# One stage in place of three between the first expert layer and the second projection of a two-layer diffusion backbone, with a shorter routing and a reordered scan end

## The chip, the cores and the metric

The kernel runs on one core of one Trainium2 chip, in float32 throughout. The metric is the device time of one execution in microseconds. TensorE, VectorE (DVE in the rows), ScalarE (ACT), GpSimd (POOL) and SyncE (SP) each run their own instruction stream and meet at semaphores. PE in the rows is TensorE's matmul, PEld its weight load. SyncE only issues transfers here; GpSimd issues the indirect ones (gathers) and ScalarE a few.

## What is computed

Two layers over 256 context tokens and 1024 latent tokens (1280, in ten tiles of 128), width 1024. What matters here of the reference:

```
# end of layer 0, tokens = context and latent
out = hier_moe(tokens, ...)          # every token: 2 of 32 experts, sorted and padded by expert
h = h + g2 * out                     # g2: a gate row of 1024, one for context, one for latent

# begin of layer 1
a = modulate(rmsnorm(h, norm_mix[1]), sh1, s1)      # rmsnorm(h) * (1 + s1) + sh1
q, k, v = split_qkv(a @ w_in)        # 1024 x 1536; context tokens: k and v only (512 columns)
q, k = axial_rope(q), axial_rope(k)  # latent tokens only
```

`hier_moe` picks a group of experts and two experts in it per token, weighs them, and evaluates each expert on its own tokens. The delta rule scan of layer 0 (`gated_delta_rule`) goes over the tiles in both directions at once, with a triangular inverse per tile and head; its values are `v_new = T (beta v - beta e^g k S)` and its state grows by `k^T (v_new * decay)`.

## The kernel before

`build` (L2499) runs stages in sequence. Each is a block: all engines start together after a barrier and end together before the next; ahead of the barrier GpSimd sets each semaphore of the new block. The order of the stages is `begin`, `norm_mod`, `project0`, `delta_scan`, `gate_heads`, `project_norm`, then `moe` (`route`, `experts`, `combine`), `norm_mod` again, `project1`, `attend`, `project_norm`, and `moe` for layer 1. The hidden state `H` stays in SBUF.

**Between the experts and attention** three blocks follow one another.

- `combine` (L1949), layer 0: for each of the ten tiles GpSimd gathers the two expert rows of every token (L1983, two gathers of 512 KB per tile, all twenty issued at once into ten buffers), ScalarE scales one (L2003), VectorE adds the other (L2031), multiplies by the gate row (L2033) and adds to `H` (L2038, on odd tiles GpSimd does it, L1987). ScalarE squares `H` with a row sum (L1999). After the last tile one mean, one root and one reciprocal serve all ten tiles (L2051 to L2053).
- `norm_mod` (L312): SyncE spreads the scale and shift rows over the partitions (L308) and loads the 6 MB of `at_w_in` (L145). Per tile VectorE makes `H * rstd * scale` (L362) and adds the shift (L365), TensorE turns it with eight transposes (L379), and ScalarE copies two half tiles to `aT`, which holds all ten tiles (L351).
- `project1` (L2072): per tile TensorE multiplies `aT` by the weights (L2136; group 2 alone for the two context tiles, groups 0, 1 and 2 for a latent tile), then turns the tile before (L2151, four transposes per group). ScalarE copies the turned tile (L2166), then the products to `z` (L2179) and the keys twice (L2190). VectorE (L2207 to L2209) and GpSimd (L2220 to L2222) rotate. SyncE stores `att_q`, `att_k` and `att_v`.

**Routing** (`route`, L1464, once per layer) is one chain on VectorE, in which each instruction waits for the one before (`st.link`). It begins when `const_ramp` has come from memory (L1504, L1554). It finds group and experts, counts by two matmuls (L1528, L1529), runs over the tiles with a position and a running count each (L1590, L1591), and finds units, slots and the rows of each block (L1594 to L1620), from which TensorE makes the index list (L1532). Meanwhile VectorE builds the table of blocks, on all partitions alike, with wide comparisons (L1624 to L1653), and copies the list (L1655). ScalarE has by then issued the 12 MB of the first two experts. `experts` starts with a gather by that list, and its further weight loads wait for the blocks that use their buffers.

**The scan** (`delta_scan`) has ten steps, with both directions `d` interleaved. Each has five merges in 64-blocks and a sixth across. What follows the merges on VectorE: `state_times_beta` and `residual` for both directions (L1003, L1008), `decay_beta` (L975), the decayed values out of PSUM (L1070) once ScalarE has copied `v_new` (L943), and `a_matrix` (L980). TensorE multiplies `TT` by `R` for both directions, then keys by keys for both (all at L1093), and turns A of the next step (`turn_a`, L1109, L1112) when `at_ready` and `vd_ready` allow.

## Time and profile before

| | us |
|---|---|
| median of 3 runs | 3668.06 (3665.86 to 3669.89) |
| the profiled execution | 3672.49 |
| its span, first to last instruction | 3670.8 |
| TensorE busy in the span | 3018.0 (82%) |
| VectorE, ScalarE, GpSimd busy | 1216.2, 676.9, 332.2 |
| mean granted TensorE clock | 0.921 |

Since the stages stand in sequence, a stage's own slowest chain sets its length, and busy shares over the whole span say little. The stages are told apart by the first and last instruction of their lines in the order of time.

### The profile page before, as it was taken

Reading aid. Unit: us, or ns where it says so; the run is one execution under the profiler, and the core shown is the slowest. Engines: PE = TensorE matmul, PEld = TensorE weight load, DVE = VectorE, ACT = ScalarE, POOL = GpSimd, SP = SyncE. Lnnn points to the kernel's source line nnn. Section 1 sums busy time; section 2 is a strip of 40 time slices with the busy share of each in tenths; the row PEclk is TensorE's granted clock in tenths of the full one; section 3 lists DMA queues with packets and bytes.
Section 4 is the critical chain, followed back from the end, with each engine's and each line's share of the span. In section 5 each row is a group of like instructions: output and inputs, shape, how many; then the busy total and the mean of one; then the engine's idle time right before and its main releaser. Section 6 shows DMA issues by size and latency. Waiting matters only on the chain. (4 is left out here: it accounts for less than half of the span.)

```text
span 3670.8 us, 51018 instructions
## 1 busy us (share of the span) xinstructions
PE 3018.0 (82%) x18238; PEld 1569.6 (43%) x18239; DVE 1216.2 (33%) x2215; ACT 676.9 (18%) x1522; POOL 332.2 (9%) x374
## 2 busy tenths in 40 slices
PE   3999998899949939999998549868889489789991
PEld 1555554788824423333333124445555333233330
DVE  3323322766672351111110242256643501001114
ACT  2312211111120100000000131156651000000002
POOL 0000001111210010000000212201110000000002
PEclk8999999999979959999999769989999699899995
DMA  6511101232236348679978330131110389886874
GB/s 273 157 50 57 50 26 50 88 97 80 66 138 220 143 181 355 272 307 378 369 290 352 143 116 35 45 123 42 52 31 35 155 343 398 331 369 248 353 291 166
DMA packets 153503, 667.47 MB, mean 182 GB/s; under 512 B 26480, under 2 KB 62864, under 8 KB 122624
## 3 DMA queue, kind: packets, MB, share of 16 engines
q1 hardware_dynamic: 125360, 545.54, 38.7%
q0 software_dynamic: 18496, 66.64, 4.9%
q10 hardware_dynamic: 9488, 53.09, 3.5%
q8 instruction: 109, 1.79, 0.2%
q14 instruction: 50, 0.41, 0.0%
HBM read 595.84 MB, written 69.39 MB: 181 GB/s over the span
## 5 line engine op out<-in xcount | busy, mean ns | idle before, releaser
L1831 PE MATMUL bank<-w,xT 128*64 x3392 | 751.5, 601 | 66.4 <-DMA w<-in_moe_w 40.8
L511 PE MATMUL bank<-aT,w 128*128 128x512 f32 (+1 forms) x1344 | 487.8, 523 | 6.7 <-DVE short L712 5.9
L1831 PEld LDWEIGHTS bank<-w,xT 128*64 128x64 f32 x3392 | 249.1, 139 | 532.6 <-issue 532.5
L1851 PE MATMUL bank<-w,hT 128*64 (+1 forms) x1696 | 380.9, 602 | 55.2 <-issue 50.0
L511 PEld LDWEIGHTS bank<-aT,w 128*128 128x128 f32 x1344 | 255.1, 191 | 227.6 <-issue 215.8
L1923 DVE TENSOR_TENSOR h<-h,bank 128x512 f32<-128x512 f32 x53 | 36.5, 688 | 785.2 <-PE bank L1831 785.2
L1851 PEld LDWEIGHTS bank<-w,hT 128*64 128x64 f32 x1696 | 122.2, 138 | 277.7 <-issue 277.7
L2136 PE MATMUL bank<-at_w_in,aT 128*128 128x512 f32 x416 | 182.3, 598 | 2.9 <-PEq L116 2.9
L2328 PE MATMUL bank<-eye,probs 128*128 128x128 f32 x640 | 99.1, 286 | 45.2 <-ACT probsT L2394 45.0
L1780 POOL DMA_INDIRECT x<-moe_x,idx_block x55 | 53.4, 970 | 841.0 <-PE bank L1807 839.3
L2136 PEld LDWEIGHTS bank<-at_w_in,aT 128*128 128x128 f32 x416 | 79.2, 192 | 99.8 <-issue 99.8
L1890 ACT COPY xT<-bank 128x512 f32<-128x512 f32 x55 | 32.2, 585 | 482.6 <-PE bank L1807 482.6
L1883 ACT ACTIVATE h<-bank 128x512 f32<-128x512 f32 x53 | 31.6, 597 | 470.4 <-PE bank L1831 470.4
L1350 PE MATMUL bank<-at_w_out,att 128*128 128x512 f32 x256 | 112.6, 599 | 3.0 <-PEq L116 3.0
L379 PE MATMUL bank<-eye,a 128*128 128x128 f32 x160 | 31.7, 368 | 100.7 <-DVE a L365 96.1
L1934 DVE COPY y<-bank 128x512 f32<-128x512 f32 x53 | 36.6, 691 | 223.3 <-PE bank L1851 223.3
L1896 ACT COPY y<-bank 128x512 f32<-128x512 f32 x53 | 31.0, 585 | 420.6 <-PE bank L1851 420.6
L2328 PEld LDWEIGHTS bank<-eye,probs 128*128 128x128 f32 x640 | 68.5, 142 | 82.0 <-ACT probsT L2394 60.5
L1929 DVE COPY hT<-bank 128x512 f32<-128x512 f32 x53 | 36.7, 692 | 194.0 <-PE bank L1813 194.0
L1350 PE MATMUL bank<-ab_w_out,oT 128*128 128x512 f32 x160 | 77.1, 627 | 24.5 <-PEq L116 24.5
L1807 PE MATMUL bank<-eye,x 128*128 128x128 f32 x440 | 65.4, 293 | 34.1 <-DMA x<-moe_x,idx_block 34.1
L1047 DVE TENSOR_TENSOR T_TT_sub<-T_TT_sub,bank 128x512 f32<-128x512 f32 x100 | 68.7, 688 | 73.6 <-PE bank L1171 73.6
(336 smaller groups left out, 3919.3 us busy)
## 6 DMA issues: line engine op xcount, KB each, us to landing
w<-in_moe_w SPq DMA_DIRECT2D x180, 2048.0 KB, 13.2
ada_w<-in_ada_w SPq DMA_DIRECT2D x48, 1024.0 KB, 8.6
moe_y<-y ACTq DMA_DIRECT2D x53, 512.0 KB, 10.4
w<-in_moe_w ACTq DMA_DIRECT2D x12, 2048.0 KB, 21.5
w<-in_ab_w_in SPq DMA_DIRECT2D x28, 512.0 KB, 3.9
moe_y<-zero POOLq DMA_DIRECT2D x1, 8192.0 KB, 24.9
moe_x<-a SPq DMA_DIRECT2D x13, 512.0 KB, 2.7
at_w_in<-in_at_w_in SPq DMA_DIRECT2D x3, 2048.0 KB, 16.6
```

The source lines that it names most:

```text
L511: mm = pe.matmul(k.bank[3 * s + n][:, 0:width], w[j][:, c, :], aT[:, c, at:at + width], start=(c == 0), stop=(c == KC - 1))
L1047: V_.tensor_tensor(X[d][:], X[d][:], both_new[d], ALU.subtract).then_inc(x_ready[d], 1)
L1350: mm = pe.matmul(k.bank[Y[n % 2] + half][:], lhs(c, t), w[:, c, half * 512:(half + 1) * 512], start=(c == 0), stop=(c == KC - 1))
L1780: pool.indirect_dma_start(x[:], None, dr["moe_x"], bass.IndirectOffsetOnAxis(ap=one[:, 0:1], axis=0)).then_inc(x_in, 16)
L1807: t = pe.transpose(k.bank[X[c // 4]][:, (c % 4) * P:(c % 4 + 1) * P], x[:, c:D:KC], k.eye[:])
L1831: mm = pe.matmul(k.bank[UP[half]][u * UNIT:(u + 1) * UNIT, :], xT[:, c, u * UNIT:(u + 1) * UNIT], w13[:, r if u else ds(buf[0], 1), half, ...
L1851: mm = pe.matmul(k.bank[Y[half]][u * UNIT:(u + 1) * UNIT, :], hT[:, c, u * UNIT:(u + 1) * UNIT], w2[:, r if u else ds(buf[0], 1), at:at + ...
L1923: nc.vector.tensor_tensor(h[:], h[:], k.bank[UP[1]][:], ALU.mult).then_inc(h_ready, 1)
L1929: nc.vector.tensor_copy(hT[:].rearrange("p c q -> p (c q)"), k.bank[HT][:]).then_inc(hT_ready, 1)
L1934: nc.vector.tensor_copy(y[:, 0:512], k.bank[Y[0]][:]).then_inc(y_dve, 1)
L2136: mm = pe.matmul(k.bank[3 * s + g][:], aT[:, c, t * P:(t + 1) * P], w[:, c, g * 512:(g + 1) * 512], start=(c == 0), stop=(c == KC - 1))
L2328: mm = pe.transpose(k.bank[6 + f % 2][:, at:at + P], pr[m % 2][:, h, c * P:(c + 1) * P], k.eye[:])
```

## The change

Three parts, and one load that moves to `begin`: the ramp is loaded there once and kept.

```diff
@@ begin: SyncE
         sp.dma_start(k.tri[:], ...).then_inc(consts_in, 16)
+        sp.dma_start(k.ramp[:], dr["const_ramp"].to_broadcast([P, P])).then_inc(consts_in, 16)
```

**Scan ends.** The decayed values move into the merges of the next step and read ScalarE's copy; one direction's residual moves into the last merge; two loops over the directions become one each.

```diff
+        def decayed_values(s, d):
+            dve.wait_ge(vn_copied[d], primed(s + 1))
+            V_.tensor_tensor(VD[d][:], VN[d][:], stat(kdec, ...), ALU.mult).then_inc(vd_ready[d], 1)
@@ VectorE, merge n of step s
+                if n == 0 and s:            # before the two subtractions of merge 0
+                    decayed_values(s - 1, 0)
                 if n == 4:
                     decayed_scores(s, 0)
+                    state_times_beta(s, 0)
                 for d in R2:
                     ...subtract(X[d])
+                    if n == 4 and d == 0:
+                        residual(s, 0)
+                if n == 0 and s:            # after them
+                    decayed_values(s - 1, 1)
@@ VectorE, after the merges
-            for d in R2:
-                state_times_beta(s, d)
-                residual(s, d)
+            state_times_beta(s, 1)
+            residual(s, 1)
             for d in R2:
                 if more:
                     decay_beta(s + 1, d)
-            for d in R2:
-                dve.wait_ge(vn_copied[d], primed(s + 1))
-                V_.tensor_tensor(VD[d][:], bank[d][P_BANK], ...).then_inc(vd_ready[d], 1)
-            for d in R2:
-                if more:
                     a_matrix(s + 1, d)
@@ TensorE
         def turn_a(s, d):
-            pe.wait_ge(vd_ready[d], primed(s))
+            pe.wait_ge(vn_copied[d], primed(s))
...
                 heads(bank[d][P_BANK], TT[d], R[d]).then_inc(vn_ready[d], 1)
-            for d in R2:
                 if s + 1 < NT:
                     key_products(s + 1, d)
```

**Routing.** No load ahead; the running counts are linked alone and the positions come from one instruction; the table is computed with one unit per partition and turned by five matmuls; the weights of the experts are computed later.

```diff
         for t in range(T):
-            st.link(V.tensor_tensor(pos[:, t], k.bank[0][...], run[:], ALU.add))
-            st.link(V.tensor_tensor(run[:], run[:], k.bank[1][...], ALU.add))
+            st.link(V.tensor_tensor(run[:, t + 1, :], run[:, t, :], k.bank[1][...], ALU.add))
+        V.tensor_tensor(pos[:], run[:, 0:T, :], k.bank[0][...], ALU.add)
@@ after at_row: L1624 to L1653 go; in their place, on [P, NE], [P, 1] and [P, 3, 11]
+        V.tensor_scalar(begun[:], incl[:], unit[:, 1:2], None, ALU.is_gt)
+        st.link(V.tensor_scalar(cmp[:], incl[:], unit[:, 0:1], None, ALU.is_le))
+        st.link(V.tensor_reduce(own[:], cmp[:], AX.X, ALU.add))
+        ...four more..., then_inc(units_owned, 1)
+        ...the six instructions L1579 to L1584, moved here...
         dve.wait_ge(listed, primed(1))
         V.tensor_copy(idx[:], k.bank[4][:, 0:NB])
+        dve.wait_ge(tabled, primed(1))
+        ...seven short copies out of banks 5 and 6 to table[0:1, ...]
@@ TensorE, after the index list
+        pe.wait_ge(units_owned, primed(1))
+        for n in range(1 + RING):
+            pe.matmul(k.bank[5][0:1, n * P:(n + 1) * P], of_unit[:, n:n + 1], k.eye[:], ...)
+        pe.matmul(k.bank[6][0:1, 0:NE], ones[:, 0:1], begun[:], ...).then_inc(tabled, 1)
```

**The joined stage.** `combine_project` takes the place of layer 0's `combine`, of `norm_mod` and of `project1`, tile by tile. Layer 1 keeps `combine`.

```diff
+    RY = 3                               # gathered tiles held
@@ SyncE, in this order: rope, two gate rows, then
+        sp.dma_start(w[:, :, 1024:1536], src[:, :, 1024:1536]).then_inc(w_in[2], 16)
+        for v in R2:
+            for n, m in enumerate((1, 0)):
+                sp.dma_start(cols[:, v, n, :], dr["mods"][1, v, m * D:(m + 1) * D].rearrange("(c p) -> p c", p=P),
+                             allow_slow_non_contiguous=True).then_inc(cols_in, 16)
+        ...w groups 0 and 1
@@ TensorE, project(t)
+            pe.wait_ge(aT_act, primed(t + 1)); pe.wait_ge(aT_dve, primed(t + 1))
+            for n, g in enumerate(groups(t)):
+                pe.wait_ge(w_in[g], primed(16))
                 ...eight products into bank 3 * s + g...
+                if n == 0 and t + 1 < NT:
+                    turn_a(t + 1)        # eight transposes, banks 6 and 7
@@ ScalarE, for t in -2 .. NT-1
+            scale(t + 2)                 # as L2003
+            copy_a(t + 1)                # four [P, 128] Identity with scale and bias columns, first waits cols_in
+            square(t + 2)                # Square with row sum, then waits mean_ready, Sqrt
             take_turned(t - 1); take_products(t); double_keys(t)
@@ VectorE, for t in -2 .. NT
+            rotate(t - 1)                # L2207 to L2209
+            add(t + 2)                   # L2031, L2033, L2038
+            copy_a(t + 1)                # four [P, 128] tensor_scalar out of PSUM
+            normalise(t + 2)             # mean, reciprocal, a = H * rstd
@@ GpSimd
+        gathers of tiles 0, 1, 2, then for t in -2 .. NT
+            rotate(t - 1)                # L2220 to L2222
+            gather(t + 5) once sum_ready(t + 2)
```

## Rows read from the trace of the kernel before

**Rows 1.** The page: its span, and the granted clock in 40 slices.

```profile
span 3670.8 us, 51018 instructions
PEclk8999999999979959999999769989999699899995
```

**Rows 2.** Timeline from combine to project1: start, length, engine, line, idle time before.

```profile
2081.96 0.80 SPq L308 DMA_DIRECT2D gate_rows<-mods  x2
...
2090.65 1.15 ACT L2003 ACTIVATE y<-y,weights 128x1024 f32<-128x1024 f32 x1 [13.23 <-DMA y<-moe_y,slots]
...
2136.64 0.22 DVE L2053 RECIPROCAL rstd<-rstd 128x10 f32<-128x10 f32 x1 [1.35 <-ACT rstd L2018]
...
2176.75 16.19 PE L2136 MATMUL bank<-at_w_in,aT 128*128 128x512 f32 x32 [2.90 <-PEq L116]
...
2193.22 20.77 PE L2136 MATMUL bank<-at_w_in,aT 128*128 128x512 f32 x48
...
2214.25 20.77 PE L2136 MATMUL bank<-at_w_in,aT 128*128 128x512 f32 x48
...
2236.68 13.90 PE L2136 MATMUL bank<-at_w_in,aT 128*128 128x512 f32 x32
```

**Rows 3.** Groups by line, 2081.9 to 2391 us: busy time, mean ns, idle before.

```profile
L2031 DVE SCALAR_TENSOR_TENSOR y<-y,weights 128x1024 f32<-128x1024 f32 x10 | 12.8, 1284 | 22.2 <-ACT y L2003 22.2
L365 DVE TENSOR_TENSOR a<-a,shift_rows 128x1024 f32<-128x1024 f32 x10 | 12.3, 1225 | 0.3
L351 ACT COPY aT<-bank 128x512 f32<-128x512 f32 x20 | 10.7, 589 | 27.6 <-PE bank L379 27.6
L1999 ACT ACTIVATE squares<-H 128x1024 f32<-128x1024 f32 x10 | 10.5, 1049 | 18.0 <-POOL H L1987 16.7 <-DVE H L2038 1.2
```

**Rows 4.** The tile conv_qkv: a one-input VectorE operation, and its loads.

```profile
L666 DVE TENSOR_SCALAR y<-x_raw,conv_qkv x12: 882/884/891, 122.8 to 571.5; 128x1282 f32<-128x1282 f32 x12
...
L448 SPq DMA_DIRECT2D conv_qkv<-in_ab_conv_qkv x3: 583/1335/5400, 92.5 to 108.7; - x3
...
DMA to landing us min/median/max: 5.0/10.1/21.1
```

**Rows 5.** Stretches: length, busy PE, PEld, DVE, ACT, POOL, clock, DMA share, GB/s.

```profile
2093.00:2096.00 3.00, 0.00 (x0) 0.00 (x0) 2.93 (x4) 1.39 (x2) 2.39 (x3) 0.50 1.03 418
...
2913.00:2918.00 5.00, 5.00 (x26) 5.00 (x25) 4.83 (x6) 0.00 (x0) 0.00 (x0) 0.50 0.16 69
```

**Rows 6.** Timeline of the routing of layer 0, GpSimd, VectorE and TensorE.

```profile
1308.65 0.20 POOL L1508 MEMSET ones<- 128x128 f32 x1 [17.17 <-POOLq L116]
...
1314.80 0.23 DVE L1555 TENSOR_SCALAR w<-w 128x128 f32<-128x128 f32 x1 [15.49 <-DMA w<-in_const_ramp]
...
1325.99 0.09 DVE L1588 MEMSET w<- 128x32 f32 x1 [1.37 <-PE bank L1529]
...
1330.79 0.82 DVE L1594 TENSOR_TENSOR w<-w 128x640 f32<-128x640 f32 x1
...
1343.30 8.75 PE L1532 MATMUL bank<-w,at_row 128*128 128x37 f32 x40 [17.46 <-DVE at_row L1620]
...
1360.47 0.20 DVE L1655 CAST idx<-bank 128x37 int32<-128x37 f32 x1
```

**Rows 7.** The same of layer 1, where it differs.

```profile
2911.94 7.05 PE L1532 MATMUL bank<-w,at_row 128*128 128x37 f32 x32 [15.08 <-DVE at_row L1620]
...
2929.12 0.20 DVE L1655 CAST idx<-bank 128x37 int32<-128x37 f32 x1
```

**Rows 8.** TensorE at the end of a scan step, timeline; VectorE's merges, 654 to 1030 us, by line.

```profile
713.16 1.09 PE L1195 MATMUL bank<-T_TT_sub,A_T_off 64*64 64x64 f32 x16 [0.33 <-DVE A_T_off L1061]
714.84 1.16 PE L1093 MATMUL bank<-R,TT 128*128 128x128 f32 x8 [0.58 <-DVE R L1008]
...
719.41 0.68 PE L1109 MATMUL bank<-eye,AT 64*64 64x64 f32 x16 [0.30 <-DVE AT L980]
...
L1047 DVE TENSOR_TENSOR T_TT_sub<-T_TT_sub,bank 128x512 f32<-128x512 f32 x100 | 68.7, 688 | 73.6 <-PE bank L1171 73.6
```

More of the change, by code:

```diff
@@ L1500, in route @@
     block = k.block()
-    @block.sync
-    def _(sp):
-        sp.dma_start(ramp[:], dr["const_ramp"].to_broadcast([P, P])).then_inc(c_in, 16)
     @block.gpsimd
@@ L1647, in _ @@
-        per = tf[:, Table.OF_BLOCK:].rearrange("p (b n) -> p b n", n=Table.PER)
-        st.link(V.scalar_tensor_tensor(out=owner[:], in0=rounds[:, 0], scalar=-float(RING), in1=owner[:], op0=ALU.mult, op1=ALU.add))
-        st.link(V.tensor_scalar(per[:, :, 0:2], owner[:].rearrange("p (b u) -> p b u", u=2), float(RING), None, ALU.add))
-        for r in range(RING):
-            st.link(V.tensor_copy(per[:, :, 2 + r], rounds[:, r, 1:U:2]))
-        st.link(V.tensor_copy(table[:], tf[:]))
+        dve.wait_ge(units_set, primed(1))
@@ L1659 @@
+        V.tensor_copy(table[0:1, Table.BLOCKS:Table.BLOCKS + 1], k.bank[6][0:1, NE - 1:NE])
+        V.tensor_scalar(table[0:1, Table.LAST:Table.LAST + 1], k.bank[6][0:1, NE - 1:NE], -1.0, None, ALU.add)
 class Ring:
@@ L1945, in _, with combine @@
         second(last)
-def combine(k, l, first, slots, wts, final=False):
+def combine(k, l, first, slots, wts):
     nc, dr, H = k.nc, k.dram, k.H
@@ L2067, in moe, with combine_project @@
         with k.scope():
-            combine(k, l, first, slots, wts, final=(l == 1))
-def project1(k, aT, weights):
-    nc, dr = k.nc, k.dram
+            after(slots, wts)
+def combine_project(k, slots, wts):
+    nc, dr, H = k.nc, k.dram, k.H
     R2 = range(2)
@@ L2097, in rounds, with groups, turn_bank, wait_bank @@
         return t if t < CT else CT + 3 * (t - CT)
+    def groups(t):
+        return (2,) if t < CT else (0, 1, 2)
+    fills = [("a", 0, 0), ("a", 0, 1)]
+    for t in range(NT + 1):
+        if t + 1 < NT:
+            fills += [("a", t + 1, 0), ("a", t + 1, 1)]
+        if t:
+            fills += [("z", t - 1, g) for g in groups(t - 1)]
+    def turn_bank(what, t, g):
+        return k.bank[6 + fills.index((what, t, g)) % 2]
+    def wait_bank(pe, what, t, g):
+        f = fills.index((what, t, g))
+        if f < 2:
+            return
+        before, u, h = fills[f - 2]
+        if before == "z":
+            pe.wait_ge(taken, primed(rounds(u) + (h if u >= CT else 0) + 1))
+        else:
+            pe.wait_ge((aT_act, aT_dve)[h], primed(u + 1))
     def stores(t):
@@ L2213, in _, with rotate @@
+        def rotate(t):
+            pool.wait_ge(z_copied, primed(t + 1))
+            pool.wait_ge(turned, primed(rounds(t - 1)))
+            lo, hi, cos, sin = halves(t)
+            nc.gpsimd.tensor_tensor(t3[:], lo, sin, ALU.mult)
+            st.link(nc.gpsimd.tensor_tensor(t4[:], hi, cos, ALU.mult))
+            nc.gpsimd.tensor_tensor(rt[t % 2][:, :, :, 1, :], t3[:], t4[:], ALU.add).then_inc(second_ready, 1)
+        for n in range(RY):
+            gather(n)
         nc.gpsimd.memset(pad[:], 0.0).then_inc(pad_set, 1)
@@ L2215, in _ @@
         st = Steps(pool, pool_order)
[L2216 to L2222 removed]
+        for t in range(-2, NT + 1):
+            if t - 1 >= CT:
+                rotate(t - 1)
+            if t + 2 + RY < NT:
+                pool.wait_ge(sum_ready, primed(t + 3))
+                gather(t + 2 + RY)
 def attend(k, att, early):
@@ L2506, in build @@
         k.silu_c = k.sb("silu_c", [P, KC, 2])
+        k.ramp = k.sb("ramp", [P, P])
         k.logits = k.sb("logits", [P, NT, GROUPS + NE])
```

314 lines of the change are left out of this document (185 added, 129 removed).

## The prediction

> **What bounds the kernel now.** I read the page first, then the timeline around the changed lines, then the groups by line and the waits of those stretches. The page gives a span of 3670.8 us [rows 1]; its execution took 3672.49, so 1.7 lie around the span. It stands 4.4 above the median of 3668.06, and I take each gain off the median. What a repeated measurement can tell from no change is about 0.2%, 7 us.
>
> The stages stand one after another, so I look for what each stage in the change waits for. Between the experts and attention TensorE multiplies nothing from 2081.96, when combine issues its first load, to 2176.75, when the first product of project1 starts [rows 2]: 94.8 us, of which combine takes 55 (to 2136.64 and its end) and norm_mod 40. Combine is bound by VectorE (2.93 busy of 3 us) with the transfers at 418 GB/s beside it [rows 5]. From 2193.22 on, project1 is TensorE's: a latent tile takes 20.77 us of products, and the next starts 22.4 after the last (2214.25 to 2236.68), so its twelve transposes cost 1.66 [rows 2]. The reader should see two different bounds in sequence, VectorE's and then TensorE's, over the same ten tiles. Routing is VectorE's chain from 1314.80 to 1360.67, after 6.15 of waiting for the ramp [rows 6]. At the end of a scan step TensorE waits three times for VectorE (0.33, 0.58, 0.30) [rows 8].
>
> **The joined stage.** Its first work starts where combine's did. GpSimd primes some 20 more semaphores before the barrier; no row shows that alone, between nothing and some 2 us I take 1.2. The first pair of gathered rows was in by 2090.65 [rows 2], with one gate load beside. Now 2.4 MB more compete for the same engines, and two queues share: I take 1.5 later, so 2093.3 (bounds 2090.6 and 2096).
>
> The first tile then goes through: scale 1.15, three VectorE operations of 1.28, 1.23 and 1.23 (3.8 with gaps), square 1.05 and its read of the sum, 0.2 (1.3), mean, table load and root, reciprocal (2.0), a = H * r. That last is one input at 0.884 for 1282 columns [rows 4], 0.71 for 1024, where norm_mod had 1.28 and 1.23 [rows 3]. Eight transposes follow on a cold TensorE (2.0) and four copies of 128 columns on either engine. A copy of 512 is 0.59 [rows 3]; four short ones I take at 1.1, for 1.3 with the wait. VectorE does the next tile's addition first (3.8), which hides transposes. Product 0 could start at 2107.3 by this chain.
>
> **But the columns.** The copies wait for four transfers of 1024 single elements, 256 per DMA engine. They stand on SyncE's queue behind the rope, gate rows and 2 MB of weights, beside three gathered tiles: 6.6 MB at 415 GB/s [rows 5] is 15.8 us from 2084, 2101 with the priming. The nearest row is conv_qkv, loaded the same way: 1536 elements landed in 5.0 us at best and 21.1 at worst, the worst beside an 8 MB store [rows 4]. Less some 2.2 of fixed latency over 96 elements per engine, that is 29 ns at best and 197 at worst. I take 29, since only one more gathered tile (2.5 us) goes beside them: 7.5 + 2.5 + 2 puts them at 2113, product 0 at 2114.2. With 197 ns it is 2153, with nothing 2107.3.
>
> By the Trainium skill (DMA: Bandwidth & Descriptors, the table of key figures) a DMA engine needs pieces of at least 512 B for its full rate. Counted as such pieces, the 4096 elements would be 2.1 MB and an estimated 5 us in place of 7.5, and the sum would be 3577.5. No row shows such pieces alone.
>
> Product 0 takes 6.86 (a third of 20.77) and 2.25 for the cold clock: project1's first sixteen products and a turn took 16.5 to 2193.22, against 14.3 [rows 2]. Then the turn of tile 1 (1.1), its copies (1.2), product 1 (6.86), turn 2 (1.1), and copies that turn 0 half hides (1.2): tile 2 starts 20.6 later, at 2134.8, where it started at 2193.22. That is 58.4 us.
>
> From there each tile pays TensorE eight transposes more. Twelve cost 1.66, so 1.1, seven times (tiles 3 to 9): 7.7 us back. **Left: 50.7.**
>
> Is TensorE still the bound? From the start of tile t's products, VectorE rotates tile t-1 by about 7.3 us, waits for ScalarE's scale (queued behind the keys of t-1, which wait for GpSimd's rotation), adds by 14.3, copies by 15.3, and has the next a by 17. The copies are needed at 23.6 and a at 30.4. So 8 us of slack cover all of this: scale, add, square, root and copies are priced at nothing there, and if the cover is gone every excess us costs eight. The gather of tile t+5 is queued behind GpSimd's rotation and the square of t+2; it has over two tiles' time. Weight groups 0 and 1 are queued behind the columns: 4.2 MB and two gathered tiles are 15 us, in by 2128, needed at 2134.8 and 2142.7. The stores and the tail after the last product stay as they are. If VectorE does become late, the copies of tile t+1 are what TensorE waits for.
>
> **The routing.** The load goes: VectorE can begin at 1308.7 in place of 1314.80, 6.1. One more small load in begin stands behind 8 MB and before stores that wait longer, nothing. The six weight instructions stood inside TensorE's counting, nothing gained by moving them. From the count on, 4.8 us (1325.99 to 1330.79) of twenty linked instructions become ten at 0.223 and one of 0.49, 2.7: 2.1 gained. The index matmuls then start at 1343.30 - 8.2 = 1335.1 and end 8.75 later at 1343.8 [rows 6]. The table has 14 short instructions under them (3 us, hidden). Behind them come five matmuls of one or 32 rows, ten passes. At the cold clock a pass of 37 columns took 8.75/40 = 0.22; of 128 columns I take 0.25: 2.4, bounded by 1 and 5. Then seven copies of one partition, 0.9: 1347.2 against 1360.67. **13.4.**
>
> Layer 1: 6.1, then 1.9 for eight tiles, so the index matmuls end at 2919.0 - 8.0 = 2911.0, the table at 2914.4 against 2929.32 [rows 7]. **14.8.** What comes next is the gather and block 0, whose weights had landed: transfers fall to 69 GB/s in 2913 to 2918 [rows 5], and block 0 needs them some 10 us later than that even now. Later loads follow the blocks that free buffers, so they shift along.
>
> **The scan.** TensorE's first product with R comes 1.68 after L1195, of which 0.58 is the wait for R [rows 8]. With the first residual made in the last merge, it waits only for ScalarE's copy, 1.14 after. Keys times keys of the same direction follow at once, so that VectorE makes A for direction 0 while TensorE does direction 1. The waits 0.17 and 0.30 go too: the turn starts 5.1 after L1195 instead of 6.25. What is late next is nothing but TensorE's own four batches of 0.99. Seven of nine boundaries look so, two run at a lower clock and are TensorE's already (0.57): 7 x 1.15 + 1.1. The last step leaves out two products' worth of VectorE work, 0.5 to 1. The moved instructions (0.69 each) go into VectorE's gaps, 0.74 on average before L1047 [rows 8] and longer in merge 0. If they don't fit they cost up to 0.7 in each of four places per step, 25 us at worst. I take **9.3**, bounded by 3 and 12.
>
> **Sum.** 50.7 + 13.4 + 14.8 + 9.3 = 88.2. 3668.06 - 88.2 = **3580**.
>
> **Rivals.**
> - *The columns cost nothing.* They land before 2107.3; for it speaks that the 5.0 of conv_qkv includes another load ahead of it. 7 us more gained: **3573**. Chance 0.18.
> - *The columns are slow.* Near the 197 ns end; against it, that figure stood beside a store at full rate all along. 10 to 39 us less: **3590 to 3619**, 3600 for the middle. Chance 0.15.
> - *VectorE or ScalarE is late in every latent tile.* GpSimd's rotation stretches VectorE's (2.2 for an operation that runs 0.83 alone in the timeline), and the added VectorE work now meets it. 2.5 us beyond the slack, eight times: 20, **3600**. Against it: those 8 us of slack. Chance 0.12.
> - *The scan or the routing doesn't do what it says*: another wait (ks_ready, the one-row matmuls) takes the removed one's place, and that part, about 10 or 28 us, stays as before: **3590 to 3608**. Chance 0.07.
> - *TensorE's clock falls, and it ends slower.* The slices that hold project1 (24 to 26 of 40) show 6, 9 and 9 tenths, the 6 with the stages before it in it [rows 1]. In the joined stage each tile has three places to wait at. At the lower of its two levels, 1.2 GHz, the latent products alone would take 8 x 20.77 = 166 us more: 3580 + 166 = **3746**. It decides from the point at which over 88/166, 53%, of them run so. Against it: TensorE is busy before each of these waits for 7 us or more. The Trainium skill (TensorE: Matmul & The Clock Gate, Part 1) tells of a kernel in which short idle gaps between groups made the clock swing between both levels. Chance 0.03.
> - Forecast, 3571 to 3590: 0.45.
>
> **The numbers.** The likeliest case gives 3580. Down to 3562 takes in the free columns with the best bounds of scan (12) and priming; up to 3605 takes in late engines, a part without effect and slow columns to their middle. Faster 0.96, within 0.2% 0.01, slower 0.03.
>
> **What would show it.** Right: in the new trace, product 0 starts 30 to 34 us after the first gather, and what ended ScalarE's idle time before its first Identity is the columns' DMA. From tile 2 on TensorE starts a tile every 23.5 us, idle only for the usual copies. The routing lasts 38.5 and 33.5 us to the list's copy, 13 to 15 less than now. In the scan the turn of A starts 5.1 after the last merge's second product. Wrong: a period over 24.5, waits of the products for weight groups 0 or 1, a granted clock below 0.9 in the stage, or gaps of VectorE in merges 0 and 4 turned into waits of TensorE.

## The result, and the profile after

The changed kernel takes **3562.4 us** in the median of four runs (3557.2 to 3563.2) against 3667.0 for the kernel before, run beside it (four runs, 3664.6 to 3669.9): a ratio of 0.9712, 95% interval 0.9695 to 0.9728. It is 104.5 us faster; 88.2 had been forecast, so 3580 was 17.6 too high, and the measured time lies at the lower edge of the range, 3562. The profiled execution took 3563.2 us, 1.7 of them outside its span; that of before took 3672.5, 5.5 above its median. So the two profiles differ by 109.3, and some 5 of that are only that this one execution of before was longer than its median.

I took the two traces apart at the same first and last products of TensorE (worked out from their timelines):

```
from ... to ...                                      before    after   less   forecast
first product of project0, first scan step's end      571.5    572.1   -0.6      -
nine scan steps                                       348.4    332.3   16.1     9.3
to the last product of project_norm, layer 0          267.0    263.2    3.8      -
routing, layer 0 (to the experts' first product)       82.1     68.0   14.1    13.4
experts, layer 0                                      703.3    705.4   -2.1      -
joined stage (to the first product of attention)      326.0    271.4   54.5    50.7
attention, project_norm                               460.9    460.9    0.0      -
routing, layer 1 (to the experts' first product)       78.3     63.0   15.3    14.8
first to second block of the experts, layer 1          25.3     18.6    6.7      -
the rest                                              704.1    702.0    2.1      -
```

Ahead of the first product lie 103.9 us in before and 104.4 in after. Which of these differences repeat is told further below.

**The joined stage.** The timeline of the changed kernel, from the experts' end (start, length, engine, line, idle time before it and what ended that):

```profile
2052.96 0.38 SPq L2121 DMA_DIRECT2D rope<-in_const_rope  x1
...
2053.66 0.95 POOL L2329 DMA_INDIRECT y<-moe_y,slots  x1 [55.80 <-POOLq L116]
...
2054.95 19.37 SPq L2129 DMA_DIRECT2D scale_shift<-mods  x4
...
2064.55 1.15 ACT L2198 ACTIVATE y<-y,weights 128x1024 f32<-128x1024 f32 x1 [17.86 <-DMA y<-moe_y,slots]
...
2073.38 1.97 PE L2156 MATMUL bank<-eye,a 128*128 128x128 f32 x8 [27.42 <-DVE a L2311]
...
2079.03 1.51 ACT L2214 ACTIVATE aT<-bank,scale_shift 128x128 f32<-128x128 f32 x4 [5.65 <-DMA scale_shift<-mods]
2079.04 1.37 DVE L2299 TENSOR_SCALAR aT<-bank,scale_shift 128x128 f32<-128x128 f32 x4 [1.82 <-DMA scale_shift<-mods]
...
2080.59 9.70 PE L2168 MATMUL bank<-at_w_in,aT 128*128 128x512 f32 x16 [5.24 <-ACT aT L2214]
...
2102.37 7.03 PE L2168 MATMUL bank<-at_w_in,aT 128*128 128x512 f32 x16
...
2147.58 7.03 PE L2168 MATMUL bank<-at_w_in,aT 128*128 128x512 f32 x16
...
2170.89 7.03 PE L2168 MATMUL bank<-at_w_in,aT 128*128 128x512 f32 x16
```

Both copying engines wait for the columns, as forecast, but these are in 25.4 us after the first gather. The forecast had them in at 2113, which is 29 after its gather (2082.68 in before, and 1.2 for priming). Product 0 starts 26.9 after that gather and tile 2 21.8 after product 0, and from tile 3 on the tiles follow each other by 23.3 (2147.58 to 2170.89; 22.4 before [rows 2]). One such tile, as a stretch (length, busy PE, PEld, DVE, ACT, POOL, clock, DMA share, GB/s):

```profile
2147.50:2170.80 23.30, 23.00 (x71) 11.20 (x70) 11.00 (x13) 7.54 (x16) 8.49 (x5) 1.00 0.25 85
```

TensorE is busy for 23.0 of 23.3 us at the full clock, VectorE for 11.0. From there on the stage is bound by TensorE. The timeline of the first routing:

```profile
1290.11 0.24 DVE L1564 TENSOR_SCALAR w<-ramp 128x128 f32<-128x128 f32 x1 [9.54 <-PEq L116]
...
1316.39 8.75 PE L1538 MATMUL bank<-w,w 128*128 128x37 f32 x40 [15.24 <-DVE w L1622]
1325.07 1.86 PE L1542 MATMUL bank<-eye,w 128*1 128x128 f32 x8
1326.73 0.31 PE L1543 MATMUL bank<-w,ones 128*1 128x32 f32 x2
...
1327.70 0.14 DVE L1653 TENSOR_SCALAR table<-bank 1x1 int32<-1x1 f32 x1
```

VectorE starts with the stage and not 6.15 us later [rows 6]; the table ends 37.8 us after the stage's start at 1290.06 (38.5 forecast).

**The scan.** The end of the same step as in [rows 8] in the changed kernel; then the stretches of the fourth and sixth of the nine steps, first in the kernel before, then in the changed one:

```profile
713.00 1.09 PE L1201 MATMUL bank<-T_TT_sub,A_T_off 64*64 64x64 f32 x16 [0.32 <-DVE A_T_off L1073]
714.21 1.13 PE L1099 MATMUL bank<-R,TT 128*128 128x128 f32 x8
715.17 1.06 PE L1099 MATMUL bank<-KT 128*128 128x128 f32 x8
716.07 1.06 PE L1099 MATMUL bank<-R,TT 128*128 128x128 f32 x8
716.96 1.06 PE L1099 MATMUL bank<-KT 128*128 128x128 f32 x8
717.95 0.68 PE L1115 MATMUL bank<-eye,AT 64*64 64x64 f32 x16
```

```profile
789.70:830.51 40.81, 38.10 (x688) 35.38 (x689) 27.06 (x47) 5.74 (x12) 6.99 (x6) 0.92 0.26 80
...
868.30:910.41 42.11, 38.18 (x688) 35.45 (x689) 27.03 (x47) 5.74 (x12) 6.98 (x6) 0.92 0.24 77
```

```profile
787.50:825.30 37.80, 34.67 (x688) 32.21 (x689) 27.07 (x47) 5.74 (x12) 6.99 (x6) 1.00 0.28 86
...
861.79:898.79 37.00, 34.84 (x689) 32.29 (x689) 26.97 (x47) 5.74 (x12) 6.99 (x6) 1.00 0.29 88
```

The three waits behind the last merge's products (0.58, 0.17 and 0.30) are down to none, and the one in front of them stays (0.32, 0.33 before), as forecast. The turn of A starts 4.95 after L1201 (5.1 forecast). The undisturbed step takes 36.49 us in place of 37.79. But two steps of before ran at a granted clock of 0.92 and took 3.0 and 4.3 us more; after has none at a lower clock.

Some steps are longer at the full clock too. In the second step of the changed kernel TensorE stops in the middle of a row of sixteen products, and the profile names nothing that it waited for:

```profile
746.09 0.45 PE L1173 MATMUL bank<-A_T_off,T_TT_sub 64*64 64x64 f32 x9
747.80 0.39 PE L1173 MATMUL bank<-A_T_off,T_TT_sub 64*64 64x64 f32 x6 [1.26 <-issue]
```

The trace has a packet of the instruction queue, 16 KB of code, from 745.39 to 746.37, and the products go on 1.4 us behind it. In the scans of the fourteen profiles there are 30 such stops of over 0.3 us (0.31 to 2.19), and each ends 1.2 to 1.6 us behind the end of such a packet. A step with a stop of over 0.5 us at the full clock is longer than the undisturbed one by the stop and some 0.3 us. By this timing they are waits for code, in a row without a branch; no run was made to test it. The steps that are longer at the full clock cost after 3.9 us in all, in the main by such stops, and before 2.6.

**A wait that the change doesn't touch.** In layer 1 the experts' second block came 7 us late in before, and the profile names nothing it waited for. First the timeline of before there, then the row of one line of the experts' code, the branches of TensorE's sequencer (count, least/median/longest in ns, first and last start), in before and in after:

```profile
2957.38 1.16 PE L1807 MATMUL bank<-eye,x 128*128 128x128 f32 x8
2958.75 0.74 PE L1813 MATMUL bank<-eye,h 128*128 128x128 f32 x4 [0.22 <-issue]
2966.51 15.52 PE L1831 MATMUL bank<-w,xT 128*64 x64 [7.02 <-issue]
```

```profile
L1798 PEldq COMPARE_BRANCH  x318: 68/200/5972, 1372.2 to 3600.3; - x159
```

```profile
L1796 PEldq COMPARE_BRANCH  x318: 68/200/450, 1339.3 to 3492.1; - x159
```

One branch of 5.97 us stands in the gap (2960.25 to 2966.22). In the changed kernel none of 318 is longer than 0.45, and the second block comes 6.7 us earlier. That is the largest single gain outside my sum.

### The profile page after: what moved, and what is told of

Read it like the earlier page. It is cut to its first block and busy times, and to the rows that moved or that the text cites. A ratio compares the mean times of both kernels' runs of the same rounds, so it can differ in the third digit from the quotient of the medians.

```text
span 3561.5 us, 51108 instructions
## 1 busy us (share of the span) xinstructions
PE 3002.3 (84%) x18258; PEld 1558.7 (44%) x18259; DVE 1186.3 (33%) x2240; ACT 682.4 (19%) x1551; POOL 322.6 (9%) x373
## 5 line engine op out<-in xcount | busy, mean ns | idle before, releaser
L1829 PE MATMUL bank<-w,xT 128*64 (+1 forms) x3392 | 750.1, 600 | 61.9 <-DMA w<-in_moe_w 42.5
L2456 PEld LDWEIGHTS bank<-eye,probs 128*128 128x128 f32 x640 | 68.4, 142 | 82.1 <-ACT probsT L2522 60.6
L1431 DVE TENSOR_TENSOR y<-bank,gate_rows 128x512 f32<-128x512 f32 x36 | 24.9, 691 | 174.9 <-PE bank L1355 174.8
L214 PE MATMUL bank<-ada_w,silu_c 128*2 128x512 f32 x384 | 52.8, 659 | 34.7 <-DMA ada_w<-in_ada_w 34.7
```

The costliest lines, as they stand in the source:

```text
L214: mm = pe.matmul(self.to(n)[self.on(q), :], self.k.silu_c[:, j, :], self.w[:, c % self.ring, q * self.NW:(q + 1) * self.NW], start=(j == 0 ...
L1829: mm = pe.matmul(k.bank[UP[half]][u * UNIT:(u + 1) * UNIT, :], xT[:, c, u * UNIT:(u + 1) * UNIT], w13[:, r if u else ds(buf[0], 1), half, ...
L2456: mm = pe.transpose(k.bank[6 + f % 2][:, at:at + P], pr[m % 2][:, h, c * P:(c + 1) * P], k.eye[:])
```

## The experiments

Each edit is given against the kernel named. The length of an undisturbed scan step repeats to 0.04 us from profile to profile, so one profile tells it; whole times scatter by several us. late_residual, keys_behind, vd_back, vector_slack, pad_after and ramp_early have one execution each, so from their whole times nothing below some 10 us is read.

**One part of the change at a time.** The change cut to one part, the rest as in the kernel before. Of each, the hunk that names the part:

```diff
--- joined_only
-        moe(k, 0, 0)
+        moe(k, 0, 0, lambda slots, wts: combine_project(k, slots, wts))
--- routing_only
-    ramp = lent.sb("ramp", [P, P])
+    ramp = k.ramp
...
+        pe.wait_ge(units_owned, primed(1))
--- scan_only
-            pe.wait_ge(vd_ready[d], primed(s))
+            pe.wait_ge(vn_copied[d], primed(s))
...
-            for d in R2:
                 if s + 1 < NT:
                     key_products(s + 1, d)
```

> The kernel before with only the joined stage; routing and scan as before. From the two profiles the stage is worth 56.3 us (the first work of the stage to the first work of attention), 5.6 more than the 50.7 forecast. Theory A, the parts add and nothing else moved: 54.5 to 58.5 us faster. Theory B, the three parts help each other or a part of the stage's gain was the layout or phase of the rest: under 52 or over 60. If the 7.0 us wait at the second block of layer 1 (seen in the profile of before, not in that of after) belongs to the joined stage, it is gone here and the gain is 60 to 64.

> The kernel before with only the routing change (the ramp loaded at the start, the table by TensorE). Forecast 28.2 us; the two profiles show 14.2 for layer 0 and 15.5 for layer 1, 29.7. Theory A, the parts add: 28 to 31 us faster. Theory B, the second block's 7.0 us wait in layer 1 ended because routing ends earlier against the weights' loads: 35 to 38 us faster, and the profile shows no such wait. Theory C, that wait is an accident of one execution: 28 to 31, whether or not the profile has it.

> The kernel before with only the scan's change. Forecast 9.3. The two profiles show 1.30 us for each undisturbed step (37.79 to 36.49), nine of them 11.7, less 1.1 for a later first step, and 4.4 more because fewer steps ran at a lower clock. Theory A, only the waits of TensorE at the step's end count: 10 to 12.5 us faster, and steps at the lower clock appear as often as before. Theory B, the shorter waits also keep the clock up (three long steps of nine before, at 0.91 to 0.96): 14 to 18 us faster, and steps of 38.7 to 42.1 us are gone.

Against 3671.5 (nine runs): joined 3614.7, ratio 0.9849 (0.9834 to 0.9864); routing 3637.8, 0.9907 (0.9892 to 0.9922); scan 3650.6, 0.9947 (0.9934 to 0.9961). Gains of 57, 34 and 21 us (intervals about 5 us to either side), together 112. All at once gave 104.5, but beside other executions of before (3667.0); in the session of these three, columns_early below, which has all three parts and its columns earlier, was 111.2 faster. So nothing here speaks against a plain sum. From the traces: the joined stage alone is worth 54.4 in its own stretch, as in the whole; its theory A holds, and the long branch is still there (6.18 us). The routing alone is worth 14.0 + 15.4 in its stretches, and the second block comes 5.1 us earlier; its longest branch is 1.73. The time lies between theory C's range (and A's) and B's, and its interval reaches both; the missing wait is B's, but why it goes is not what B says, as the next runs show. The scan alone has the step of 36.49, no step at a lower clock, and the long branch (5.95): theory B in what the trace shows, with nine steps 15.2 us shorter than in the profile of before; the 21 in the medians is above B's 14 to 18, and its interval (14 to 24) holds them.

**Where the branch comes from.** Products whose results nobody reads, in time when TensorE has nothing to do:

```diff
--- pad_before, on the kernel before
         mm.then_inc(listed, 1)
+        for n in range(4):
+            pe.matmul(k.bank[5][0:1, n * P:(n + 1) * P], ones[:, n:n + 1], k.eye[:], start=True, stop=True)
+        pe.matmul(k.bank[6][0:1, 0:NE], ones[:, 0:1], strict[:, 0:NE], start=True, stop=True)
--- pad_after, on the changed kernel
         pe.matmul(k.bank[6][0:1, 0:NE], ones[:, 0:1], begun[:], start=True, stop=True).then_inc(tabled, 1)
+        for n in range(24):
+            pe.matmul(k.bank[7][0:1, 0:8], ones[:, n:n + 1], ones[:, 0:8], start=(n == 0), stop=(n == 23))
```

> The kernel before, with five small products added to TensorE's part of each routing, behind the index products, where TensorE has nothing else to do for over 17 us; their results are not used. In the three profiles with the old routing a branch of TensorE at the second block of layer 1 took 5.97 to 6.18 us, while a 16 KB piece of code came in behind the weights' transfers; with the new routing it took 0.44, 0.44 and 1.73. Theory A, the branch waits for code, and where the pieces begin decides it: the added instructions move all code behind them about as the new table does, the branch takes under 2 us, the second block starts 18 to 21 us after the first in place of 25.3, and the time is 4 to 8 us below before. Theory B, the long branch comes from the old routing's timing (what VectorE and the transfers do): it stays at about 6 us, the second block at 25 us, and the time is that of before within 2 us.

> The changed kernel with 24 one-column products behind the table's in each routing, in time that TensorE has free. Theory A, a branch of TensorE is long where the piece of code behind it has to come in beside the weights, so it depends on how much code stands before it: another branch in the experts or the same one can be long now, over 1 us, or none, and the time moves by no more than 0 to 8 us with it. Theory B, the new table or its timing keeps the branches short whatever the position: none over 0.5 us.

The branches' rows of pad_before and of pad_after:

```profile
L1801 PEldq COMPARE_BRANCH  x318: 67/200/1334, 1371.3 to 3596.0; - x159
```

```profile
L1798 PEldq COMPARE_BRANCH  x318: 68/200/5984, 1343.5 to 3517.2; - x159
```

Ten useless products in the two routings of before take the long branch away: 1.33 us, and the second block comes 20.55 after the first, not 25.26. In the changed kernel 48 useless products bring back not one but three long branches, 5.63 at 1362.1, 5.98 at 1829.7 and 5.65 at 2876.2, and the kernel takes 3588.7, 26 us more than after; the three branches account for 17.3. The transfer queues of before in 2963.5 to 2965.0, inside its branch (packets, MB, share of 16 engines):

```profile
q1 hardware_dynamic: 39, 0.43, 66.7%
q0 software_dynamic: 39, 0.16, 27.0%
q8 instruction: 1, 0.02, 4.0%
```

Beside weights and rows it holds one packet of 16 KB of code (at 2963.85, 0.96 long), and the branch ends 1.4 us behind it; from 2960.3 to 2963.5 the same view has none. There are seven branches of over 5.5 us, one each in before, joined_only, scan_only and ramp_early and three in pad_after, and during each such a packet comes in, 3.2 to 3.8 us after its start. In routing_only and pad_before (1.73 and 1.33) the last packet had started 1.4 us ahead of the branch. All nine end 1.4 to 1.5 us behind the end of the packet, as the stops in the scan do. So theory A is borne out in its mechanism: the branch goes to code that isn't there yet, and how much code stands before it decides which branch it is. Its bound on the time was wrong: pad_after moved by 26 us in its one execution, where 0 to 8 had been expected. Of time, pad_before shows less than it should: 3663.5 against 3665.0, ratio 0.9995 (0.9986 to 1.0005), at most 5 us of gain where the trace has 4.7 at that place. 1.6 of them are lost again by the last block; how much of the rest is scatter isn't told apart.

**The scan's three moves, undone one by one** in the changed kernel:

```diff
--- late_residual
                     decayed_scores(s, 0)
-                    state_times_beta(s, 0)
...
-                    if n == 4 and d == 0:
-                        residual(s, 0)
...
-            state_times_beta(s, 1)
-            residual(s, 1)
+            for d in R2:
+                state_times_beta(s, d)
+                residual(s, d)
--- keys_behind
                 heads(bank[d][P_BANK], TT[d], R[d]).then_inc(vn_ready[d], 1)
+            for d in R2:
                 if s + 1 < NT:
--- vd_back
-                if n == 0 and s:
-                    decayed_values(s - 1, 0)
...
                 if more:
                     decay_beta(s + 1, d)
+            for d in R2:
+                decayed_values(s, d)
+            for d in R2:
+                if more:
                     a_matrix(s + 1, d)
...
-            pe.wait_ge(vn_copied[d], primed(s))
+            pe.wait_ge(vd_ready[d], primed(s))
```

> The changed kernel, with the state's product with beta and the residual of direction 0 moved back behind the last merge. An undisturbed scan step took 37.79 us before and 36.49 after. Theory A (the forecast's), the wait of 0.58 for R is what the early residual removes, and it is back: 37.1 to 37.3 a step. Theory B, the other moves cover it: under 36.8.

> The changed kernel, with the keys' products of the next step put behind both directions' products with R, as before. Theory A, the order matters, since VectorE can then make A for direction 0 only while TensorE has nothing but direction 1's keys: 0.2 to 0.5 us more a step, 36.7 to 37.0. Theory B, the moved VD operations alone had removed the wait of 0.30: 36.5. Together with the run before, what is left of 1.30 when both are undone belongs to the VD operations taken from behind the residuals.

> The changed kernel with the decayed values made behind the residuals again, ahead of A, and the turn of A waiting for them. Steps: 36.49 in after, 37.00 with the residual late, 36.60 with the keys behind, 37.79 before. Theory A, the three parts add up to 1.30: 37.1 to 37.3 here. Theory B, they overlap, and each alone is worth less than it is together: under 36.9.

Undisturbed steps: late_residual 37.00, keys_behind 36.60, vd_back 37.75, against 36.49 and 37.79. The residual is worth 0.51, 0.1 under theory A's range and 0.2 above B's (the forecast's wait for R was 0.58). The order of the keys alone is worth 0.11, between the two theories. And vd_back loses 1.26 of 1.30: both of its theories are wrong. Its timeline, at the same place:

```profile
723.65 1.06 PE L1099 MATMUL bank<-KT 128*128 128x128 f32 x8
723.85 0.59 ACT L944 COPY v_new<-bank 128x512 f32<-128x512 f32 x1 [0.86 <-PE bank L1099]
...
724.47 0.69 DVE L1008 TENSOR_TENSOR R<-v_new,k_decay 128x512 f32<-128x512 f32 x1 [0.68 <-ACT v_new L944]
725.08 1.28 DVE L981 TENSOR_TENSOR AT<-decay_beta,bank 128x512 f32<-128x512 f32 x2
725.91 0.68 PE L1115 MATMUL bank<-eye,AT 64*64 64x64 f32 x16 [1.20 <-DVE AT L981]
```

With the keys of direction 0 in between, direction 1's new values come later; VectorE, which now makes the decayed values ahead of A, waits 0.68 for ScalarE's copy of the new values, and TensorE waits 1.20 for A. So the decayed values must leave this place for the other two moves to be worth anything: the three are not a sum.

**The columns.** Loaded in the first routing, where SyncE has nothing to do:

```diff
--- columns_early: moe of layer 0, called by SyncE in route
+            def load(sp):
+                for v in range(2):
+                    for n, m in enumerate((1, 0)):
+                        sp.dma_start(k.cols[:, v, n, :], k.dram["mods"][1, v, m * D:(m + 1) * D].rearrange("(c p) -> p c", p=P),
+                                     allow_slow_non_contiguous=True).then_inc(k.cols_in, 16)
--- combine_project
-        for v in R2:
-            for n, m in enumerate((1, 0)):
-                sp.dma_start(cols[:, v, n, :], dr["mods"][1, v, m * D:(m + 1) * D].rearrange("(c p) -> p c", p=P),
-                             allow_slow_non_contiguous=True).then_inc(cols_in, 16)
```

> The changed kernel with the four column transfers moved from the joined stage to the first routing, over 700 us before they are needed. In the profile of after both copying engines waited for them: ScalarE 5.65 us, VectorE 1.82 behind its own addition. Theory A, they cost what VectorE's own wait says: 1.8 us faster than after. Theory B, they also hold back the weights and rows that share the engines with them: 3 to 6 us faster than after, product 0 starts 23 us after the first gather in place of 26.9. Theory C, weight group 2 lands no earlier than the columns did, and it is the next wait: 0 to 1 us faster.

3560.3 us (3557.6 to 3571.8, five runs), 0.9704 of before (0.9687 to 0.9721), where after had 0.9712: by the times not told apart. In the trace product 0 starts 25.5 us after the first gather in place of 26.9, and the stage is 2.4 shorter (269.0 for 271.4). That is between theories A and B. What then holds product 0 is VectorE's own order: its copies stand behind the addition for tile 1.

**A faster start.** On top of early columns:

```diff
--- start_up: SyncE, and VectorE's loop over the tiles
+        spread_row(k, sp, g_rows[:, 0, :], 0, 0, 5, g_in)
...
+        sp.wait_ge(y_in[0], 32)
         sp.dma_start(w[:, :, 1024:1536], src[:, :, 1024:1536]).then_inc(w_in[2], 16)
+        sp.wait_ge(y_in[1], 32)
+        spread_row(k, sp, g_rows[:, 1, :], 0, 1, 5, g1_in)
...
+            if t == -1:
+                copy_a(0)
+            if t == 0:
+                dve.wait_ge(g1_in, primed(16))
             if t + 2 < NT:
                 add(t + 2)
```

VectorE and GpSimd wait for the rope where they first use it.

> The changed kernel with the columns loaded in the first routing, and the joined stage's start in another order: the first gather competes with one gate row alone; weight group 2 waits for it, the other gate row and the rope for the second; VectorE copies the first tile's columns ahead of its addition for the second. Product 0 came 26.9 us after the first gather in after and 25.5 with early columns. Theory A, the transfers and VectorE's addition bound the start: 19 to 22 us, 4 to 6 us faster than columns_early, some 3555. Theory B, weight group 2 becomes what the first product waits for: 23 to 25 us, 0 to 2 us faster. Theory C, a later second tile gives it back: the third tile's products start no earlier.

3556.1 us (3552.8 to 3558.1, five runs), ratio 0.9700 (0.9687 to 0.9714) to the kernel before (3665.0, 15 runs). Timeline:

```profile
2052.06 0.95 POOL L2348 DMA_INDIRECT y<-moe_y,slots  x1 [55.03 <-POOLq L116]
...
2059.18 1.15 ACT L2212 ACTIVATE y<-y,weights 128x1024 f32<-128x1024 f32 x1 [14.10 <-DMA y<-moe_y,slots]
...
2071.46 9.65 PE L2182 MATMUL bank<-at_w_in,aT 128*128 128x512 f32 x16 [1.50 <-DVE aT L2313]
...
2093.18 7.03 PE L2182 MATMUL bank<-at_w_in,aT 128*128 128x512 f32 x16
```

The first rows are in after 7.1 us and not 10.9; product 0 starts 19.4 after the gather, theory A, and tile 2 keeps it (21.7 later). The stage is 264.1 us, 7.3 less than in after. It has the lowest median of the kernels run, 6 us below after's. The two were run in different sessions, and the intervals of their ratios overlap; that it is faster than after rests on the 7.3 us in the trace.

**How much slack VectorE has.** Nine more multiplications a tile, whose result nobody reads:

```diff
--- vector_slack: combine_project, then add(t)
+    EXTRA, waste = 9, k.sb("waste", [P, D])
...
             V.tensor_tensor(H[:, t, :], H[:, t, :], y[:, s, 1, :], ALU.add).then_inc(h_added, 1)
+            for n in range(EXTRA if t > CT else 0):
+                st.link(V.tensor_tensor(waste[:], g_rows[:, 0, :], g_rows[:, 1, :], ALU.mult))
```

> The changed kernel with nine more multiplications of 1024 columns on VectorE behind the addition of each tile from the fourth on (seven tiles). In the trace of after VectorE's copies of the next tile end 7.7 us before TensorE wants them, in a period of 23.30. Nine at 1.23 to 1.27 are 11.2 us. Theory A, VectorE has 7.7 us of slack in each tile and is late by the rest: the period of those tiles is 26.5 to 27.5, the stage 22 to 28 us longer. Theory B, TensorE was waiting for VectorE already: the period grows by the whole 11.2. Theory C, more is hidden than that: under 25.

The timeline of TensorE at tile 2 and at one of the later tiles, and the row of its waits for VectorE in 2098 to 2330 us (us in total, times, longest):

```profile
2110.18 8.91 PE L2169 MATMUL bank<-at_w_in,aT 128*128 128x512 f32 x16 [9.92 <-issue]
...
2161.01 1.12 PE L2185 MATMUL bank<-eye,rotated 128*128 128x128 f32 x4 [4.96 <-DVE aT L2302]
2161.92 1.06 PE L2185 MATMUL bank<-eye,k_twice 128*128 128x128 f32 x4
2162.77 8.16 PE L2169 MATMUL bank<-at_w_in,aT 128*128 128x512 f32 x16
```

```profile
PE bank L2185 <- DVE aT L2302: 19.1, 5, 5.0
```

The period is 28.4 to 28.8, above theory A's range and far below B's 34.5. TensorE waits 3.8 us a tile for VectorE: 11.3 less 7.7 is 3.6, theory A's amount. The rest is the clock: the sixteen products behind each wait take 7.9 to 9.1 us for 7.03, at a granted 0.86 in 2162.77 to 2170.90, and from tile 3 on the clock falls to its lower level five times, each time during one of the five waits or within 1.1 us behind it. And tile 2 was 9.9 late, since VectorE's copies for it stand behind the lengthened addition of tile 3, and the short tile 1 gives no slack for that. Together the stage is 40.7 us longer than in after, beyond theory A's 22 to 28.

**The ramp alone**, in the kernel before:

```diff
--- ramp_early: begin
+        sp.dma_start(k.ramp[:], dr["const_ramp"].to_broadcast([P, P])).then_inc(consts_in, 16)
--- route
-        sp.dma_start(ramp[:], dr["const_ramp"].to_broadcast([P, P])).then_inc(c_in, 16)
...
-        dve.wait_ge(c_in, primed(16))
```

> The kernel before with only the ramp loaded at the start. Forecast 6.1 for each routing, nothing for the load in the first stage. Theory A: from the last product of each projection to the experts' first, 82.1 becomes 76.0 and 78.3 becomes 72.2. Theory B, ScalarE or TensorE holds the routing's start too: less than 5 each. The branch at the second block of layer 1 stays long, since no instruction of TensorE is added: about 6 us.

The routings become 75.8 and 72.2 (82.1 and 78.3 before): 6.3 and 6.1, theory A. The long branch stays, 5.87 us. So of the 29.4 us in the two routings 12.4 are the ramp and 17.0 the table.

## Why the prediction was right or wrong

**Right in kind.** The direction, the bound of each stage and the order of the parts' sizes held. Every mechanism that the sum counted is in the trace: the joined stage runs at TensorE's pace, both routings lost the ramp's 6 us and the table's chain, the three waits at the step's end are gone. Of the signs named ahead, the routings' lengths (37.8 and 33.0 us, against 38.5 and 33.5) and the turn of A (4.95 against 5.1) came in; product 0 came earlier than the 30 to 34 us named. No product waited for a weight group, and the granted clock was 1.00 from 2085.8 us on, in tile 0, to behind the last product of the projection; the two steps at a lower clock in the scan of before are another matter.

**Wrong by 16 us, in four places.** The steps that failed are two. The first is the term for the scan, 9.3 with a bound of 12, where the two profiles differ by 16.1: it counted the waits in seven of nine steps and took the lower clock in the other two as fixed. The second is the second block of layer 1's experts: the term for what follows the routing was nothing ("they shift along"), and 6.7 us of a wait of 7.0 went there. The other two places are under 4 us each. That 3562.4 still touches the range's end is luck: what the forecast names for that end (free columns 6.9, scan 12 in place of 9.3, priming 1.2) reaches only 3569, and none of its rivals holds the measured time.

- *The branch, 6.7.* Not in the sum at all. I wrote of layer 1 that what comes next is the gather and block 0, and later loads "shift along". The 7.0 us before block 1 stood in the trace with nothing named as its cause; I took it to be fixed. The runs show a branch waiting for a piece of code, moved by the position of the code. A blind forecast could hardly have had its size, but it could have widened the range by it, both ways: pad_after has 17.3 us of such branches.
- *The scan, 9.3 against 16.1 in the two profiles.* The undisturbed step lost 1.30 and not 1.15, and that in all nine, not seven: 11.7. "Two run at a lower clock and are TensorE's already" was the wrong step: in the changed kernel those steps run at the full clock. The clock is 5.7 us of the 16.1, and what longer steps cost at the full clock, in the main stops for code, takes 1.3 back (3.9 in after, 2.6 in before). What the clock cost in the five profiles with before's scan, without the stops in the same steps: 5.7, 1.1, 4.7, 2.0 and nothing. In the six with the new scan, and in the two that undo the residual or the keys alone, no step is at a lower clock; in vd_back, whose step is as long as before's, one is (0.96). Eight of the twelve stretches at the lower level begin 1.9 to 2.3 us behind the start of the last merge's second products (L1195 in before), right behind the wait for R. The mean of the five is 2.7 us, and that much of the gain I put down to the clock; that the waits bring it down is what these counts say, and no run shows it directly. The written-out sum was uneven as well: 7 x 1.15 + 1.1 is 9.2, and the 0.5 to 1 for the last step would come on top.
- *The joined stage, 50.7 against 54.5.* Product 0 came 2.9 us earlier against the experts' end than summed: the columns landed 25.4 and not 29 us after the gather, while the barrier and the gather's own start cost 1.7 more than before (1.2 taken). Tile 2 gave back 1.2. Then eight more transposes a tile cost 0.9 and not 1.1 in seven tiles: 1.6. The stage's tail was 0.6 shorter. The rival in which the columns cost nothing was nearer: they cost 1.5 us at product 0 and 2.4 over the stage, where my sum had them hold product 0 by 6.9. The price of an element was not what mattered: VectorE's copy had its own addition in front of it, and was ready only 1.82 us before they came. By the Trainium skill (DMA: Bandwidth & Descriptors, Specifications: at least 512 B a transfer for the full rate), with an estimated 5 us for the elements where I had 7.5, the sum would have been 3577.5; 2.5 us in the right direction. No run prices the elements by themselves, nor the 2.2 us of fixed latency that the sum took off. A third of 20.77 is 6.92, too, and not the 6.86 written for products 0 and 1.
- *The routings, 28.2 against 29.4.* The five products of the table took 2.0 us (1325.07 to 1327.04) and not 2.4, and the rest is spread; 0.1 was a slip in the sum (2929.32 less 2914.4 is 14.9, not 14.8).

Together 1.2 + 3.8 + 2.4 (the step) + 2.7 (the clock) + 6.7 = 16.8, against 16.3 in the medians. Of the table's other differences, the 3.8 in front of the first routing and the 2.1 of layer 0's experts are scatter for the most part: the stretch of project_norm has 2.4 more in before and in columns_early than in after, and layer 0's experts take 702.9 to 705.8 with the changed routing (pad_after's long branches aside).

**The slack of VectorE** held: 8 us forecast, 7.7 in the trace, and vector_slack shows the lateness set in there. That an excess would cost "eight times" its size was too little: here the clock also fell at each of the five waits, and 3.8 us of waiting made 5.1 to 5.5 of the period. The Trainium skill (TensorE: Matmul & The Clock Gate, Part 1) tells of a clock that swings with short gaps; in the joined stage itself no row shows it (1.00 from 2085.8 us to the last product), in vector_slack (0.86 behind a wait) and in the scan of before (0.92 in two steps) the rows do.

**Still open:** which instructions the late pieces of code hold and why some come in time and others don't, what beside the three branches (17.3) the 26 us of pad_after are, and why steps with the waits lose the clock in some executions and not in others.

## What to carry to other kernels

Read a wait that the profile puts down to nothing, in a stretch full of transfers or in the middle of a row of products, as a possible wait for code: look there at the sequencer's branches and at when the last packet of the instruction queue ended, and allow for it in a range whenever a change moves the code of a kernel with branches. Where two waits follow each other on one engine, undoing one tells little about the other: of the three moves here, undoing one alone lost 1.26 of the 1.30 us. A short wait of TensorE costs more than its length when the clock drops with it (3.8 us of waiting cost 5.1 to 5.5 a tile in vector_slack).

## What the runs showed of the hardware

- A branch of TensorE to code that isn't loaded took 5.6 to 6.2 us, seven times in the fourteen profiles, while the transfers ran at 364 to 423 GB/s; the other branches of the same line took 0.07 to 0.45, but for two of 1.73 and 1.33.
- Code seems to come late without a branch too: TensorE made 30 stops of 0.31 to 2.19 us with no releaser in the scans of the fourteen profiles, each ending 1.2 to 1.6 us behind the end of a packet of code.
- Four transfers of 1024 single elements held SyncE's queue for 19.4 us beside 6 MB of other transfers (one of them for 13.8), so the two weight groups behind them were issued that much later. But without them a plain weight load of 2 MB held the queue for 14.6 us at the same place (columns_early), so it is not the single elements alone. It cost nothing here, since the first of the two groups was needed over 30 us later.
- Sixteen products of 512 columns took 7.03 us in an unbroken row and 7.9 to 9.1 behind a wait of 3 to 5 us.
